# Hybrid decoder layer on one core: tile 0's attention first, its routing inside the attention of the first part

## What is computed

```
xn   = rms_norm(h, norm1_g)
q, k, v, ga, gg = split(xn @ w_in)          # 4 heads, each with two score maps
# attention, causal, ALiBi slopes per head
p    = softmax(s * scale + bias)            # for both maps c = 0, 1
a    = p[c=0] - lam * p[c=1];  o = a @ v;  attn = rms_norm(o, sub_g) * (1 - lam_init)
# conv group: GLU -> causal depthwise conv, 31 taps -> groupwise norm -> silu
h    = h + concat(attn, conv) @ w_out
# expert FFN, per token: 8 heads
xn2  = rms_norm(h, norm2_g);  q = xn2 @ wq[head]
s    = q . subkeys  (2 x 128 keys);  top 16 of each, then top 16 of the 256 sums -> 16 experts
ffn += gate * gelu(u_tab[e] . xn2) * v_tab[e]       # rows fetched from a table of 16384
y    = rms_norm(h + ffn, final_norm_g)
```

## Time and profile before

| | us |
|---|---|
| median of 3 runs | 3050.84 (3049.5 to 3053.46) |
| profiled execution, its own time | 3048.28 |
| span of that execution, first to last instruction | 3046.5 |
| PE busy | 2329.2 (76%) |
| DVE busy | 2079.3 (68%) |
| ACT busy | 1363.4 (45%) |
| POOL busy | 1186.2 (39%) |
| mean granted clock of TensorE | 0.853 |
| HBM read / written | 1139.03 MB / 15.41 MB |

### The profile page before, as it was taken

One profiled execution on the slowest core, in us unless ns is written; L12 is line 12 of the kernel. 1 busy time (PEld: TensorE's weight loads), 2 busy tenths in 40 slices (PEclk: granted clock), 3 DMA queues, 4 the chain that ended last, 5 costly groups with the idle time before them and its releaser, 6 DMA issues.

```text
span 3046.5 us, 36181 instructions
## 1 busy us (share of the span) xinstructions
PE 2329.2 (76%) x11968; PEld 869.6 (29%) x11968; DVE 2079.3 (68%) x5054; ACT 1363.4 (45%) x4021; POOL 1186.2 (39%) x1078
## 2 busy tenths in 40 slices
PE   9877688877788788887778777777777777777665
PEld 6554322223233233332222222212222222222211
DVE  5763566687687787767867666666666666666664
ACT  2145344444545545544544444444444444444433
POOL 1010334444444343443444444443444444444442
PEclk9987898888899999998979788878878888877876
DMA  6010899999999999999999999999999999999997
GB/s 233 34 63 19 331 426 425 426 426 426 424 414 374 396 386 420 398 399 395 417 391 427 426 426 426 426 427 425 423 426 424 426 421 419 426 427 425 423 424 315
DMA packets 174604, 1156.82 MB, mean 380 GB/s; under 512 B 20481, under 2 KB 25153, under 8 KB 40913
## 3 DMA queue, kind: packets, MB, share of 16 engines
q0 software_dynamic: 149168, 1078.73, 85.1%
q1 hardware_dynamic: 25248, 75.79, 6.4%
HBM read 1139.03 MB, written 15.41 MB: 379 GB/s over the span
## 4 chain that ended last, share of the span: by engine, by line
DMA 37%; PE 28%; ACT 11%; DVE 9%; issue 4%; POOL 1%; DVEq 0%; POOLq 0%; ACTq 0%
DMA ring<-table,e_even 20%; DMA ring<-table,e_odd 17%; PE acc L1844 14%; PE qq_ps L1817 6%; DVE ring L1604 5%; PE acc L1939 2%; ACT diag L1331 2%; ACT weight L1324 2%; ACT L1424 2%; PE proj L1791 2%; ACT L1317 1%; ACT gelu L1424 1%; DVE wide L1619 1%; PE acc L1888 1%; ACT wide L1355 1%
## 5 line engine op out<-in xcount | busy, mean ns | idle before, releaser
L1844 PE MATMUL acc<-ring,diag 64*64 64x512 f32 x8192 | 1318.9, 727 | 638.5 <-ACT diag L1331 618.6
L1127 POOL DMA_INDIRECT ring<-table,e_even x512 | 591.1, 1155 | 785.1 <-PE acc L1844 714.5
L1127 POOL DMA_INDIRECT ring<-table,e_odd x512 | 569.4, 1112 | 760.8 <-PE acc L1844 720.9
L1604 DVE CUSTOM_DVE_ANT_0 ring<-ring,xn_even 128x1024 f32<-128x1024 f32 x512 | 626.5, 1224 | 324.2 <-DMA ring<-table,e_even 163.5
L1604 DVE CUSTOM_DVE_ANT_0 ring<-ring,xn_odd 128x1024 f32<-128x1024 f32 x512 | 626.0, 1223 | 311.4 <-DMA ring<-table,e_odd 153.7
L1424 ACT ACTIVATE gelu<-dots 128x1 f32<-128x1 f32 x1024 | 205.5, 201 | 1219.6 <-DVE dots L1604 1211.4
L1844 PEld LDWEIGHTS acc<-ring,diag 64*64 64x64 f32 x8192 | 245.7, 148 | 1426.2 <-ACT diag L1331 1235.7
L1331 ACT ACTIVATE diag<-pairs,weight 128x64 f32<-128x64 f32 x1024 | 356.1, 348 | 33.5
L1817 PE MATMUL qq_ps<-wq_rest,xnT_cur 128*128 128x256 f32 x736 | 220.1, 438 | 0.0
L1817 PEld LDWEIGHTS qq_ps<-wq_rest,xnT_cur 128*128 128x128 f32 x736 | 144.7, 212 | 148.4 <-issue 131.2
L1324 ACT ACTIVATE weight<-gelu,gate_even 128x1 f32<-128x1 f32 x512 | 150.7, 294 | 16.7
(11 more groups left out here) (267 smaller groups left out, 2242.9 us busy)
## 6 DMA issues: line engine op xcount, KB each, us to landing
wide<-w_units SPq DMA_DIRECT2D x26, 512.0 KB, 8.9
wq_rest<-wq SPq DMA_DIRECT2D x11, 1024.0 KB, 9.4
ring<-table,e_even POOLq DMA_INDIRECT x512
ring<-table,e_odd POOLq DMA_INDIRECT x512
w_own<-w_units SPq DMA_DIRECT2D x10, 512.0 KB, 6.8
h_next<-x SPq DMA_DIRECT2D x8, 512.0 KB, 17.7
wide<-w_out SPq DMA_DIRECT2D x2, 2048.0 KB, 8.9
wide<-w_out SPq DMA_DIRECT2D x1, 4096.0 KB, 16.3
```

What stands on the lines that cost most here:

```text
L1127: pool.indirect_dma_start(out=ring[:, g % RING, :], out_offset=None, in_=table[:, :], in_offset=bass.IndirectOffsetOnAxis(ap=e_row[m % 2][ ...
L1604: dve.tensor_tensor_reduce(ring[:, g % RING, 0:D], ring[:, g % RING, 0:D], xn[(m // PH) % 2][:], 1.0, 0.0, ALU.mult, ALU.add, dots[:, k:k ...
L1844: ins = pe.matmul(acc[ACC_OF[t]][ROWS[j], HALF[i]], diag[ROWS[i], g % DIAGS, :], ring[ROWS[i], g % RING, D + j * 512:D + (j + 1) * 512], s ...
```

## The change

In the first part the units are taken in the order `UN`: tile 0 of all four heads first, then tiles 1 to 3 of each head. The head norm therefore runs over five groups (`END` = 4, 7, 10, 13, 16): tile 0 of all heads, then three tiles of each head. All eight filler products and the whole conv are moved ahead of the loop, `normalise_late` into it, and the five value products are split (two, one, two) with means and variances between them. Inside an iteration DVE now has biased(a) before difference(a-1), and ACT has exponentials(a) before weights_out(a-1). PE gets tile 0's projection in iterations 2 and 7, the transposes of tile 0's normed row in 9, queries of expert head 0 in 10 and of head 1 in 13, keys in 13 and 15; DVE gets the residual and norm in 8 and the search parts in 13, 14 and 15 and behind the loop. The second part starts at once with the gathers. The buffers that this needs are made outside of both parts (`shared_work`), g2 and the query weights of expert heads 1 and 2 are loaded in the first part.

The core of the diff:

```diff
+        UN = [(h, 0) for h in range(HEADS)] + [(h, i) for h in range(HEADS) for i in range(1, EARLY)]
+        END = [HEADS + (EARLY - 1) * n for n in range(HEADS + 1)]
...
@@ sync, first part
+            sp.dma_start(w.g2_row[:], g2.rearrange("(a n) -> a n", a=1).to_broadcast([P, D])).then_inc(shared["route_in"], 16)
+            for h in (1, 2):
+                sp.dma_start(w.wq_early[:, h - 1], wq[h]).then_inc(w.b_wq[h - 1], 16)
...
@@ scalar, first part
             for a in range(NU + 1):
+                if a < NU:
+                    exponentials(a)
+                if a == 1:
+                    channel_output(3)
                 if a >= 1:
                     weights_out(a - 1)
+                if a - 1 in END:
+                    head_root(END.index(a - 1))
+                if a == 8:
+                    square_0()
+                    root_0()
+                elif a == 11:
+                    expert_queries(0)
+                elif a == 12:
+                    expert_queries_t(0)
+                elif a == 13:
+                    expert_queries(1)
+                elif a == 14:
+                    expert_queries_t(1)
                 if a >= 1:
                     output_out(a - 1)
+                if a == 9:
+                    for b in range(2):
+                        transposed_0(b)
+                elif a == 15:
+                    gate_exp_0()
...
@@ vector, first part
             taps(1, 0, 8)
-            normalise_late()
             centre(0)
...
+            divide(2)
+            taps(3, 16, TAPS)
+            centre(3)
+            late_factor()
+            difference_factor()
             for a in range(NU + 1):
+                if a - 2 in END:
+                    head_output(END.index(a - 2))
+                if a == 8:
+                    residual_0()
+                if a < NU:
+                    biased(a)
+                if a == 0:
+                    divide(3)
                 if a >= 1:
                     difference(a - 1)
...
+                if a - 1 in END:
+                    head_sums(END.index(a - 1))
+                    head_scale(END.index(a - 1))
+                if a in (1, 2, 3, 4):
+                    normalise_late(2 * a - 2, 2 * a)
+                elif a == 8:
+                    norm_0()
+                elif a == 13:
+                    dve.wait_ge(w.b_const, 2)
+                    for part in range(5):
+                        route_part(dve, w, s_ps, 0, part)
+                elif a == 14:
+                    for part in range(5, 11):
+                        route_part(dve, w, s_ps, 0, part)
+                elif a == 15:
+                    for part in range(11, 16):
+                        route_part(dve, w, s_ps, 0, part)
+            head_sums(HEADS)
+            gates_0()
+            head_scale(HEADS)
+            for part in range(4):
+                route_part(dve, w, s_ps, 1, part)
+            head_output(HEADS)
+            for part in range(4, 6):
+                route_part(dve, w, s_ps, 1, part)
...
@@ tensor, first part
-            for m in range(EARLY + 1):
+            for m in range(2):
                 values(m)
+            group_means(0)
+            values(2)
+            group_variances(0)
+            for j in (G[2], A[2]):
+                for n in range(2):
+                    seg(j, n)
+            for m in range(3, EARLY + 1):
+                values(m)
+            group_means(1)
+            for n in range(2):
+                seg(Q[0], n)
+            group_variances(1)
+            for j in (G[3], A[3], Q[1]):
...
             group_means(2)
+            for n in range(2):
+                seg(K[2], n)
             group_variances(2)
+            for j in (Q[2], K[3], Q[3]):
+                for n in range(2):
+                    seg(j, n)
+            group_means(3)
+            group_variances(3)
             for a in range(NU + 1):
                 if a < NU:
                     scores(a)
                 if a >= 1:
                     transposes(a - 1)
-                if a < len(FILLERS):
-                    seg(*FILLERS[a])
+                if a == 2:
                     for c in range(CG):
                         project_tile_0(HEADS + c, first=(c == 0))
+                elif a == 7:
+                    for h in range(HEADS):
+                        project_tile_0(h, last=(h == HEADS - 1))
+                elif a == 9:
+                    transpose_0()
+                elif a == 10:
+                    expert_queries(0)
+                elif a == 12:
+                    expert_queries_t(0)
+                elif a == 13:
+                    key_scores(0)
+                    expert_queries(1)
+                elif a == 14:
+                    expert_queries_t(1)
+                elif a == 15:
+                    key_scores(1)
+                if a - 1 in END:
+                    transposed_head(END.index(a - 1))
                 if a >= 1:
                     output(a - 1)
...
@@ sync, second part
-            sp.dma_start(g2_row[:], g2.rearrange("(a n) -> a n", a=1).to_broadcast([P, D])).then_inc(b_g2, 16)
-            sp.dma_start(wq_rest[:, 0], wq[1]).then_inc(b_wq[0], 16)
+            sp.dma_start(wq_rest[:, 0], wq[3]).then_inc(b_wq[2], 16)
             mix(2)
-            for h in range(2, 6):
-                sp.dma_start(wq_rest[:, h - 1], wq[h]).then_inc(b_wq[h - 1], 16)
+            for h in range(4, 6):
+                sp.dma_start(wq_rest[:, h - 3], wq[h]).then_inc(b_wq[h - 1], 16)
```

More of the change, by code:

```diff
@@ L185, in mixer_phase @@
         act_at = {s: i + 1 for i, s in enumerate(by_act)}
-        sc_at = [2 * sum(len(chunks(a % EARLY)) for a in range(n)) for n in range(NU + 1)]
+        sc_at = [2 * sum(len(chunks(i)) for h, i in UN[:n]) for n in range(NU + 1)]
         own_use = {j: 1 + [i for i in LOADS if OWN_SLOT.get(i) == OWN_SLOT[j]].index(j) for j in OWN_SLOT}
@@ L194, in slot, with group @@
             return w_own[:, OWN_SLOT[j]]
+        def group(a):
+            n = sum(end <= a for end in END)
+            return n, a - (END[n - 1] if n else 0), END[n] - (END[n - 1] if n else 0)
         def weights_in(j):
@@ L767, in transposes @@
                     pe.wait_ge(p_ats, a)
-                    if a > EARLY:
-                        pe.wait_ge(p_ho, (a - 1) // EARLY)
+                    if a > END[0]:
+                        pe.wait_ge(p_ho, sum(end < a for end in END))
                 else:
@@ L805, in project_tile_0, with transpose_0, expert_queries, expert_queries_t @@
                 for b in range(2):
-                    pe.matmul(banks[b][:], mix_t[:, k, :], w_out_s[:, k, b * 512:b * 512 + 512], start=first, stop=last)
+                    ins = pe.matmul(banks[b][:], mix_t[:, k, :], w_out_s[:, k, b * 512:b * 512 + 512], start=first,
+                                    stop=last)
+                if last:
+                    ins.then_inc(p_proj, 1)
+            def transpose_0():
+                pe.wait_ge(w.b_xn, 1)
+                for k in range(KC):
+                    ins = pe.transpose(banks[k // 4][:, (k % 4) * P:(k % 4 + 1) * P], w.xn[0][:, k * P:(k + 1) * P],
+                                       ident[:])
+                    if k % 4 == 3:
+                        ins.then_inc(w.b_xT, 1)
+            def expert_queries(r):
+                if r == 0:
+                    pe.wait_ge(w.b_xTs, 2)
+                    pe.wait_ge(shared["route_in"], 48)
+                    weights = shared["wq0"]
+                else:
+                    pe.wait_ge(w.b_wq[0], 16)
+                    pe.wait_ge(w.b_qTs, r)
+                    weights = w.wq_early[:, r - 1]
+                for k in range(KC):
+                    ins = pe.matmul(q_ps, w.xnT[:, k, :], weights[:, k, :], start=(k == 0), stop=(k == KC - 1))
+                ins.then_inc(w.b_q, 1)
+            def expert_queries_t(r):
+                pe.wait_ge(w.b_qs, r + 1)
+                for p in range(2):
+                    ins = pe.transpose(qT_ps[:, p * P:(p + 1) * P], w.q_s[:, p * QH:(p + 1) * QH], ident[:])
+                ins.then_inc(w.b_qT, 1)
+            def key_scores(r):
+                pe.wait_ge(w.b_qTs, r + 1)
+                if r == 0:
+                    pe.wait_ge(p_root, CG)
+                else:
+                    pe.wait_ge(w.b_r, ROUTE_STEPS * (r - 1) + 3)
+                for p in range(2):
+                    ins = pe.matmul(s_ps[:, p * KEYS:(p + 1) * KEYS], w.qT_s[:, p, :], shared["keys"][:, 2 * r + p, :],
+                                    start=True, stop=True)
+                ins.then_inc(w.b_s, 1)
             pe.wait_ge(p_ws, 1)
@@ L1694, in divide @@
                 dve.tensor_tensor(yc, yc, y[:], ALU.mult).then_inc(c_dve, 1)
-            residual(0, 0)
-            residual(0, 1)
-            variance(0)
-            factor(0)
-            dve.wait_ge(b_g2, 16)
-            normalise(0)
-            for part in range(16):
-                route(0, part)
```

(8 more changed lines are left out.)

593 lines of the change are left out of this document (295 added, 298 removed).

## The result

The changed kernel takes 3075.07 us (median of 4 runs, 3074.12 to 3075.6) against 3050.41 (4 runs, 3049.5 to 3053.46): 1.0079 times as long, 95% interval 1.0061 to 1.0096. Its profiled execution spans 3073.0 us, 26.5 more than before. The forecast of 3074 held.

The account below looks back on a forecast made before the run. Full DMA engines during the gathers were taken as the bound, earlier work only shifting them. First gather +18.6 us and weights +8.5 gave +27: 3075 profiled, 3078 as median, taken as 3074, range 3060 to 3088.

Parts of the forecast that it names:

- What sets the time: Whole program: 1024 gathers of 1 MB fill the DMA engines at 426 GB/s; earlier work only shifts that train.
- Up to the loop: First part before attention: the loop's first `biased` starts at 189 us, against 182.7 before; bounds 183 and 196.
- the three waits: DVE after `centre(0)`: about 3 us behind `values(2)`, 5.5 behind G2, A2 and two values, 3 behind Q0.
- The serial chain: Attention loop: A, B, C and the next scores run in series; 101 us at higher clock, 130.3 at lower.
- A: Loop unit's scores and bias: 2.6, 3.3, 4.4 us for tiles 1, 2, 3 at the lower clock.
- B: Difference of the unit before, on DVE: 1.2 us for tile 3, smaller tiles 1.1, 0.95, 0.8.
- C: Transposes, copy out and value product of the unit before: tile 3 3.9 us, tile 2 3.25, lower clock.
- Rival 2: Attention loop: units overlap as before, 5.7 us each; first gather near 319, time 3042; chance 0.08.
- The clock: Loop: clock high for a fifth of it, first gather at 355; 324 if high throughout, 363 if low.
- Tile 0's work: In the loop, mostly on PE's chain: projection, queries, transposes, keys, search; 24 us at higher clock, 33 at lower.
- The boundary: Between the parts: 4.4 us from the last copy to the next block, where the gather can be issued at once.
- The weights: Second part's start: 3.9 MB of weights, mix tile and gain beside the first gathers cost 8.5 us; bounds 0 and 9.2.

Follow-up runs that it names:

- run 1: Changed kernel with both old orders put back: DVE difference(a-1) before biased(a), ACT weights_out(a-1) before exponentials(a); 3038.97 us, ratio 0.995 to the kernel before.
- run 2: Changed kernel with only DVE's old order put back, difference(a-1) before biased(a); 3049.93 us, ratio 0.9998 to the kernel before.
- run 3: Changed kernel with only ACT's old order put back, weights_out(a-1) before exponentials(a); 3068.97 us, ratio 1.0073 to the kernel before.
- run 6: Changed kernel with three unused 256-column PE products per loop unit, placed before the transposes; 3058.78 us, ratio 1.0036 to the kernel before.
- run 4: Changed kernel without loading 3 MB of query weights (expert heads 3, 4, 5) at the second part's start, output differs; 3067.04 us, ratio 1.0052 to the kernel before.
- run 7: On top of run 1, query weights of expert heads 4 and 5 (2 MB) loaded during the first part; 3029.86 us, ratio 0.9947 to the kernel before.
- run 9: On top of run 1, five gathers issued in the first part after its search, into slots over first-part memory; 3044.51 us, ratio 0.999 to the kernel before.
- run 10: As run 9, with one small buffer moved ahead so the five slots shift 32 bytes and are aligned; 3026.23 us, ratio 0.9927 to the kernel before.

## Why the prediction was right, step by step

- **What sets the time.** As put: what happens before the gathers shifts them, and behind the 17th gather the train keeps its length (1.7 us of 26.5). In every run but the one with misplaced slots that rest lies within 9 us of 2680.
- **Up to the loop.** Forecast 189 for the first `biased`, it was 184.87. `centre(0)` near 82 came at 82.02, and the three waits behind it, put at 3, 5.5 and 3 us, measured 3.1, 5.6 and 2.7. The last mean was done at 180.6 and not at 184.5: PE was 2 us ahead of my count before it (Q1 done near 149.4, not 151.5), and a half unit took 3.56 us where I put 3.7 (my own 0.24 per pass gives 3.8). The result lies within the bounds of 183 and 196.
- **The serial chain.** This was the step that decided, and runs 1 to 3 show its cause. A, B and C of tiles 3, 2 and 2 were put at 4.4, 1.1 and 3.25 and measured 4.4, 1.1 and 3.7, of which 0.6 are query transposes that were priced elsewhere. The sum leaves out the last unit's B, 1.2 us. Rival 2, units that overlap as before, was priced at a first gather of 319 and a time of 3042; run 1 is that rival made true, with 318.2 and 3039 (that it meets the 319 to 1 us is partly luck, for the loop's start and the boundary were off there too). Its condition was stated for PE's order alone; the runs show that the locks are VectorE's order first and ScalarE's second.
- **The clock.** Taken near the lower bound, as if a fifth were high; 0.61 is that fifth (0.5 plus a fifth of the way to 1.0). The fifth was estimated from four bursts of 4 to 9 us; that it was met so closely is in part luck. Run 6 confirms the price. That transposes count less for it, which the Trainium skill's page "TensorE: Matmul & The Clock Gate" says in "Part 4: PE-mode transpose", no run here separates.
- **Tile 0's work.** The projection's two bursts were put at 14.5 to 16.8 together and took 18.1 (8.80 and 9.27), each starting at the lower clock; the two query bursts took 5.00 and 4.82, between the bounds of 5.5 and 11.5 together. From the first `biased` to the end of the last copy 160.5 us passed, where the terms come to 161.6; since the projection alone took more than its upper bound, other terms must have come in lower than put, and no row here says which.
- **The boundary.** Taken at 4.4 us from the last copy to the gather; it was 7.2. SP's first DMA came in time (4.5), but POOL's first gather 2.7 later. This cost wasn't foreseen.
- **The weights.** 8.5 forecast, 8.7 measured; runs 4 and 7 take off 6.6 and 5.8 us of it, where the bytes they spare give 7.4 and 5. The Trainium skill's page "DMA: Bandwidth & Descriptors" says in "Issuing engines are not separate DMA queues" that the transfers of all issuers interleave on the same 16 engines. The trace agrees: bytes that simply add would cost 9.2.

The errors at the loop's start (4.1 too late) and at the boundary (2.8 too early) nearly cancel, which is luck; the total of the first gather, 355 against 352.5, is better than its parts.

The change's idea, tile 0's work under attention, was sound. Run 1 hides that work and is 13 us faster than before on its chip (3051.92); two reorderings that came with it cost 34 us at the gather.

## What to carry to other kernels

When a software pipeline is rearranged, write one iteration as a single path through all engines' queues and ask at each step whether the piece of iteration a-1 stands ahead of or behind the piece of iteration a: in these engine lists, work for the older iteration that feeds other engines belonged first. Test such orders together as well as one by one: here 20.0 and 0.05 us became 34.4. And when the work ahead of a bandwidth-bound train gets shorter, look at once at what now starts beside the train, and whether the train itself could start earlier.

## What the runs showed of the hardware

- **Where a gather lands.** Gathers of 8 KB per partition with five of eight slots 32 bytes off a multiple of 64 ran at 421 GB/s in the stretch 2000 to 3000, against 425 with all slots aligned; 19 us over the program (runs 9 and 10, which differ in the place of one 32-byte buffer and of what it shifts). Only this one offset was tried, and all fast slots start at a multiple of 256, so the runs don't tell which multiple counts. The clock was 0.79 and 0.82 in that stretch; the DMA engines were full in both.
- **The first gather.** Where POOL's first gather of the program stood unblocked at a part's start, it came 2.7 to 2.8 us behind SP's first DMA (changed kernel, run 1). Where POOL had waited for the search, it followed the search's end by 0.3 us (before, and run 9), and run 9's next gather, across the boundary, came 0.6 behind SP's first DMA (319.69 and 319.05). I read this as a one-time cost of some 2 us ahead of the program's first gather that an earlier wait hides; no run was made to test that, nor what it consists of.
- **The clock's price.** A loop at 0.61 instead of 0.81 cost 14 us in 160 (run 6 against the changed kernel), and some 16 without the wait that run 6 adds. The clock falls by a quarter and the loop grows by a tenth. In the changed kernel PE is busy for 78 of the 121 us between 189 and 310; while it waits, the chain runs through VectorE and ScalarE.
